# Hybrid decoder trunk on one NeuronCore: another order of the chains around a delta-rule head, and another bank for one part of the mixer's output stage

## The reference

```python
def gated_deltanet_mixer(h, w_in, conv_w, a_log, dt_bias, o_gain, w_out):
    p = h @ w_in
    qkv = jax.nn.silu(causal_depthwise_conv(p[..., :GDN_QKV], conv_w))
    q, k, v = split(qkv);  z, b_logit, a_logit = split(rest of p)
    q = l2_norm(heads_to_chunks(q)) * (GDN_DK ** -0.5)
    k = l2_norm(heads_to_chunks(k))
    ...
    a = strict_lower(kb @ k^T * decay)                  # per chunk
    sol = triangular_solve(a + eye, [v * beta, kb * exp(gc)])
    qk = lower(q @ k^T * decay)
    def step(state, inp):                               # scan over the chunks
        v_new = u_c - w_c @ state
        o = qd_c @ state + qk_c @ v_new
        state = state * cd_c + kd_c^T @ v_new
    o = rms_norm(o, o_gain) * silu(z)
    return o @ w_out
# layer:  x = x + rms_norm(mixer(rms_norm(x)));  x = x + rms_norm(ffn(rms_norm(x)))
```

## Time and profile before

| | |
|---|---|
| time, median of 3 runs | 2989.35 us (2988.05 to 2990.46) |
| time of the profiled execution | 2988.55 us |
| span of its records | 2986.8 us |
| TensorE matmul busy | 2766.5 us (93% of the span) |
| VectorE busy | 1555.9 us (52%) |
| ScalarE busy | 870.7 us (29%) |
| GpSimd busy | 712.1 us (24%) |
| mean granted TensorE clock | 0.965 of full speed |

### The profile page before, as it was taken

The page is one execution under the profiler, slowest core; times in us unless marked ns, Lnnn a source line. Parts: engine busy times, 40 slices in busy tenths (PEclk is TensorE's granted clock), DMA queues, the critical chain, the costliest instruction groups (busy, mean ns, idle before and its releaser), DMA issues. The chain is left out here.

```text
span 2986.8 us, 35606 instructions
## 1 busy us (share of the span) xinstructions
PE 2766.5 (93%) x13277; PEld 2282.7 (76%) x13277; DVE 1555.9 (52%) x1821; ACT 870.7 (29%) x1229; POOL 712.1 (24%) x350
## 2 busy tenths in 40 slices
PE   6789988889889999999998699999989999999996
PEld 4677777778767888888887487787778888888885
DVE  4455545555245445444454675567454444544546
ACT  5244443443433111111111434344531111111112
POOL 2423233333502222222221011111402222222221
PEclk8799999999999999999999799999999999999998
DMA  3010110100332111111111310110521111111112
GB/s 108 22 43 28 35 42 21 42 28 22 113 106 92 43 49 49 42 42 56 49 49 42 128 36 22 49 49 32 169 84 57 45 53 49 49 49 43 49 63 99
DMA packets 59109, 168.04 MB, mean 56 GB/s; under 512 B 6097, under 2 KB 19985, under 8 KB 59041
## 3 DMA queue, kind: packets, MB, share of 16 engines
q1 hardware_dynamic: 59040, 167.14, 16.6%
HBM read 143.49 MB, written 23.63 MB: 56 GB/s over the span
## 5 line engine op out<-in xcount | busy, mean ns | idle before, releaser
L191 POOL TENSOR_TENSOR f_wlo<-f_raw,f_whi 128x1024 fp32r<-128x1024 f32 x130 | 331.2, 2557 | 1101.4 <-ACT f_whi L211 1101.4
L211 ACT ACTIVATE f_whi<-f_raw 128x1024 fp32r<-128x1024 f32 x130 | 137.6, 1058 | 934.1 <-PE f_down L72 425.8
L70 PE MATMUL f_down<-f_whi,f_hhi 128*128 128x512 f32 x704 | 282.7, 402 | 19.5 <-issue 15.6
L250 DVE TENSOR_TENSOR acc<-f_down,acc 128x512 f32<-128x512 f32 x320 | 217.0, 689 | 134.3 <-PE f_down L72 134.3
L70 PE MATMUL banks<-x_hi,f_whi 128*128 128x512 f32 x704 | 276.5, 393 | 10.5 <-PEq L61 10.5
L72 PE MATMUL f_down<-f_whi,f_hlo 128*128 128x512 f32 x704 | 279.4, 397 | 0.0
L71 PE MATMUL f_down<-f_wlo,f_hhi 128*128 128x512 f32 x704 | 278.7, 396 | 0.0
L70 PE MATMUL f_up<-x_hi,f_whi 128*128 128x512 f32 x704 | 276.4, 393 | 2.1 <-POOL f_wlo L191 2.0
L71 PE MATMUL f_up<-x_lo,f_whi 128*128 128x512 f32 x704 | 276.2, 392 | 0.0
L72 PE MATMUL f_up<-x_hi,f_wlo 128*128 128x512 f32 x704 | 276.1, 392 | 0.0
L71 PE MATMUL banks<-x_lo,f_whi 128*128 128x512 f32 x704 | 275.8, 392 | 0.0
(11 more groups left out here) (433 smaller groups left out, 5476.1 us busy)
## 6 DMA issues: line engine op xcount, KB each, us to landing
f_raw<-in_ffn_w_up SPq DMA_DIRECT2D x88, 512.0 KB, 3.5
f_raw<-in_ffn_w_down SPq DMA_DIRECT2D x44, 512.0 KB, 3.5
g_raw<-in_gdn_w_in SPq DMA_DIRECT2D x32, 512.0 KB, 3.5
l_raw<-in_gla_w_in SPq DMA_DIRECT2D x24, 512.0 KB, 3.5
after_ffn_xt<-x_mid SPq DMA_DIRECT2D x16, 512.0 KB, 4.3
first_xt<-in_x SPq DMA_DIRECT2D x8, 512.0 KB, 8.0
g_columns<-cum_rows SPq DMA_DIRECT2D x8, 512.0 KB, 3.9
g_outraw<-in_gdn_w_out SPq DMA_DIRECT2D x8, 512.0 KB, 6.8
```

The lines of the kernel that those rows point to most:

```text
L70: pe.matmul(out, w_hi, x_hi, start=first, stop=False)
L191: pool.tensor_tensor(w_lo[k][:, :], raw[k][:, :], w_hi[k][:, :].bitcast(F32), ALU.subtract) \
L211: act.activation(w_hi[slot(c)][:, :], raw[slot(c)][:, :], ACT.Copy).then_inc(s_hi, 1)
L250: dve.tensor_tensor(part, down_ps[b % 4][:, :], part, ALU.add).then_inc(s_free, 1)
```

## The change

Two things are changed. In the DeltaNet's heads, the output chain of head h-1 is put ahead of the query chain of head h on every engine. On ScalarE the Silu of q leaves the scan and stands after the copy and squares of the scan's output; the last eviction of a head (`evict(h-1, 3, 1)`, the second half of the tile that the fourth projection writes, a Silu of the gate z) stands behind the first chunk's copy of the next scan; the Square of the queries and the high part of weight 3 stand behind the scaling of the output. On TensorE the turn of the queries leaves the scan and follows the first join. On GpSimd the low part of weight 2 is made ahead of the spreading, in head 0 alone. In the output stage DVE adds all E parts ahead of the first norm, and the fourth part goes to the PSUM place of the second one, after tile E.

```diff
@@ mixer_tail
     def m_ps(t):
         if t < E:
-            return (late_ps, *(x.rearrange("p k t -> p (k t)") for x in turned[::-1]))[t % 3]
+            return (late_ps, *(x.rearrange("p k t -> p (k t)") for x in turned[::-1]))[t if t < 3 else 1]
         return part_ps if (t - E) % 2 == 0 else late_ps
@@ Vector.passes
             def add(t):
-                dve.wait_ge(s_m, t + 1)
+                dve.wait_ge(s_m, t + 1 if t < 3 else t + 2)
@@
             dve.wait_ge(s_kept, 2 * E)
-            add(0)
+            for t in range(E):
+                add(t)
             dve.wait_ge(s_gain, 32)
             for t in range(NT + 2):
-                if t + 1 < E:
-                    add(t + 1)
                 if t <= E:
                     m_normed(t)
@@ Tensor.passes
-            for t in range(E + 1):
+            for t in (*range(min(E, 3)), E, *range(3, E)):
                 pe.wait_ge(s_llo, (KT - early) * (1 if t < NT // 2 else 2))
                 if 3 <= t < E:
-                    pe.wait_ge(s_add, 2 * (t - 2))
+                    pe.wait_ge(s_add, 2 * (t - 1))
...
                 if t == E + 1:
-                    pe.wait_ge(s_add, 2 * E)
+                    pe.wait_ge(s_add, 2)
@@ gdn, GpSimd
             def body(h):
                 split(h, 1)
                 near_blocks(h)
+                if peeled(h):
+                    split(h, 2)
                 spread(h, 0)
                 spread(h, 1)
                 coupling(h, 0)
-                split(h, 2)
+                if not peeled(h):
+                    split(h, 2)
@@ gdn, ScalarE, scan
-                              5: lambda: evict(h, 1, 0),
-                              6: lambda: silu(qT, 3 * h + 2)}
+                              5: lambda: evict(h, 1, 0)}
                 for n in range(NT):
...
+                    if n == 0 and projects and not peeled(h):
+                        evict(h - 1, 3, 1)
                     if n in beside:
                         beside[n]()
-                if projects:
-                    act.wait_ge(s_qtok, h + 1)
-                    act.activation(wTn[:, :, :], by_chunk(pm), ACT.Square).then_inc(s_qsq, 1)
-                    evict(h, 1, 1)
-                    if not final(h):
-                        high(h, 3)
@@ gdn, ScalarE, prepare
                 if not peeled(h):
                     output_copy(h - 1)
+                    output_squares(h - 1)
+                silu(qT, 3 * h + 2)
+                evict(h, 1, 1)
                 m1_copies(h, 0)
-                if not peeled(h):
-                    output_squares(h - 1)
-                act.wait_ge(s_qss, h + 1)
-                act.activation(stdq[:, :], ssq[:, :], ACT.Sqrt, bias=eps[:, 0:1]).then_inc(s_qstd, 1)
                 if not peeled(h):
                     output_deviation(h - 1)
                     output_norm(h - 1)
+                act.wait_ge(s_qtok, h + 1)
+                act.activation(wTn[:, :, :], by_chunk(pm), ACT.Square).then_inc(s_qsq, 1)
+                if not final(h):
+                    high(h, 3)
+                act.wait_ge(s_qss, h + 1)
+                act.activation(stdq[:, :], ssq[:, :], ACT.Sqrt, bias=eps[:, 0:1]).then_inc(s_qstd, 1)
                 evict(h, 2, 0)
...
                     key_deviation(h + 1)
-                    evict(h, 3, 1)
@@ gdn, VectorE, prepare
+                if not peeled(h):
+                    output_sums(h - 1)
+                    output_norm(h - 1)
+                join(h, 0)
+                dve.wait_ge(s_silu, 3 * h + 2)
+                dve.tensor_tensor(qdT[:, :, :], by_chunk(qT), from_start[:, :, :], ALU.mult).then_inc(s_qd, 1)
                 dve.wait_ge(s_qsq, h + 1)
                 dve.tensor_reduce(out=ssq[:, :], in_=wTn[:, :, :], axis=AX_X, op=ALU.add).then_inc(s_qss, 1)
-                if not peeled(h):
-                    output_sums(h - 1)
-                dve.tensor_tensor(qdT[:, :, :], by_chunk(qT), from_start[:, :, :], ALU.mult).then_inc(s_qd, 1)
-                join(h, 0)
-                if not peeled(h):
-                    output_norm(h - 1)
                 conv_v(h, (1,))
@@ gdn, TensorE
             def queries_by_token(h):
                 pe.wait_ge(s_silu, 3 * h + 2)
-                pe.wait_ge(s_at, h + 1)
@@ prepare
                 pe.wait_ge(s_first, 2 * h + 2)
-                pe.wait_ge(s_qsq, h + 1)
+                pe.wait_ge(s_at, h + 1)
                 coupled(h, 0)
...
                 joined(h, 0)
+                queries_by_token(h)
                 some(17, 18)
                 if not peeled(h):
+                    pe.wait_ge(s_qsq, h + 1)
                     output_turn(h - 1)
                 some(19)
                 if not peeled(h):
                     pe.wait_ge(s_og, h)
+                else:
+                    pe.wait_ge(s_qsq, h + 1)
                 coupled(h, 1)
@@ first_scan, and scan's last chunk
-                queries_by_token(0)
...
-                    if c == NT - 1:
-                        queries_by_token(h)
```

## The result

| | before | changed kernel |
|---|---|---|
| time, median | 2989.86 us (2988.05 to 2990.46, 4 runs) | 2944.17 us (2941.23 to 2947.63, 4 runs) |
| ratio, 95% interval | | 0.9849 [0.9832, 0.9866] |
| span of the profiled execution | 2986.8 us | 2939.5 us |
| first and last scan begin at | 162.20 and 790.03 us | 148.46 and 743.11 us |

The changed kernel is faster by 45.7 us. The forecast was 2945.0 with a range of 2924 to 2966, and it was right. That it is off by only 0.8 us is luck: the four runs of the changed kernel lie 6.4 us apart, and the interval of the ratio is worth 5 us to either side.

The account below looks back on a forecast made before the run. TensorE works nearly throughout, so only its waits and the low clock behind them can give. Six loop heads 24.6, head 7 6.7, head 0 13, output stage 0: 44.3 off 2988.55 gives 2944.3, plus 0.8 to the median: 2945, range 2924 to 2966.

Parts of the forecast that it names:

- First chunk: Start of a loop head's scan: the 1.58 us wait goes, a state wait of 0.8 to 0.95 comes; net -0.63.
- Last chunk and first join: Loop head: a 2.5 us wait for GpSimd's mask replaces 3.16 on ScalarE; the join starts 3.6 us earlier.
- Portion 16: After the first join: TensorE comes at 380.6 and waits for weight 2's low part until 381.15.
- The output turn: Loop head, after portions 17 and 18: the 3.67 us wait before the output's turn is gone.
- a sign of being wrong: At the second join: a wait over 5 us or stretched GpSimd operations; or clock at 0.50 over 10 us a head.
- step 5: Loop head's second join: squares, high part 3, low part 3, mask, one convolution meeting; 3.1 us wait, start 5.8 us earlier.
- Clock: Low clock behind the new waits of 2.5 and 3.1 us: 2.0 us a head charged, 0.3 given back.
- neither rival on the clock: New waits keep the clock and meet no DVE operation, 2921, chance 0.12; low clock takes back most, 2973, chance 0.16.
- Head 7: Last head, no weight 3: only DVE's gate of the output holds TensorE; 8.2 less 1.5 for clock, 6.7 us gained.
- Head 0: Low part's wait goes, 8 us comes before the second join at 118; query-key products at 131.5; gain 13, bounds 8 and 17.
- The prediction's terms from 118 on: Head 0: second join and products 5.3, low clock 2.3, DVE 0.7, third join, products and portion 5.7 us.
- Output stage: TensorE starts tile 5 earlier but waits longer for DVE's chain of norms: gain 0, between -2 and +1 us.

Follow-up runs that it names:

- Experiment 5: The changed kernel with the gate's second-half eviction back at its old place on ScalarE, ahead of the first chunk's copy: 2950.18 us, ratio 0.9870.
- experiment 6: The changed kernel with GpSimd's second mask moved ahead of low part 3: 2938.11 us, ratio 0.9826.
- experiment 8: The changed kernel with the output gate ahead of the first value convolution on VectorE, alone: 2936.21 us, ratio 0.9828.
- Experiment 10: The kernel of experiment 9 with GpSimd's first mask held back, except in head 0, until ScalarE evicted the queries' second half: 2908.92 us, ratio 0.9729.
- experiment 2: The changed kernel with the output stage of before, so the heads' part of the change alone: 2944.99 us, ratio 0.9852.
- experiment 3: The kernel before with one edit: in head 0 GpSimd makes the low part of weight 2 ahead of the spreading: 2974.44 us, ratio 0.9950.
- experiment 4: The changed kernel without head 0's early low part of weight 2 on GpSimd: 2958.56 us, ratio 0.9892.
- experiment 1: The kernel before with only the output stage's part of the change: 2990.6 us, ratio 1.0003.
- experiment 9: The changed kernel with GpSimd's first mask ahead of both spreads, second ahead of low part 3, and VectorE's output gate ahead of the first value convolution: 2918.24 us.

## Why the prediction was right

By its own steps, before the last scan: 46.92 us gained (790.03 to 743.11), 44.3 forecast. The numbers in brackets are the forecast's.

1. *First chunk.* The 1.58 us went, and the state came late by 0.65 instead of 0.8 to 0.95. Experiment 5 puts 6.0 us on this step over seven heads.
2. *Last chunk and first join.* The wait for the mask is 2.52 us (2.5), on GpSimd, in every loop head.
3. *Portion 16* waits 0.33 us (0.55) for the low part of weight 2.
4. *The output turn* starts at 368.42 with no wait, as forecast.
5. *Second join.* 2.84 us (3.1), at the end of the chain named, with one meeting of GpSimd and VectorE paid: low part 2.38, mask 3.33. Right in size, but thin in its reason. I took the mask for the only thing that held this join in a loop head. Experiments 6 and 8 show that the gate was 1.0 us behind it, so that removing one wait gives only what the other leaves. I had seen the gate for head 7 alone. The prediction named stretched operations of GpSimd at this join as a sign of being wrong, and the mask is stretched, to 3.33 from 2.36 us. By its letter that sign came true; but step 5 had itself charged 1.2 us for one such meeting, and 1.0 was paid, so the sign was worded against the step.
6. *Clock.* Charged 2.0 us a head. The six loop heads average 86.46 us, the one without low clock 84.82: 1.64 a head. That one, head 3, in whose times the steps were worked out, gained 6.24 us, against 5.8 + 0.3 = 6.1 ahead of the clock's charge. The waits of 2.5 and 2.8 us led to it in five heads of six, one or two stretches each, so neither rival on the clock came true. Experiment 10 has neither these waits nor the low clock, and a head takes 80.5 to 80.7 us in it.

A loop head gained 4.50 us on average (27.0 for six, 24.6 forecast): the clock cost less than charged. Head 7 gained 6.16 (6.7), but 2.2 in experiment 2, at another clock, so the agreement there is luck.

*Head 0* gained 13.74 us (13). The second join waits 7.80 us (8) and starts at 117.27 (118); the query-key products start at 131.33 (131.5). The prediction's terms from 118 on add up to 14.0 us and so to 132.0, not 131.5, and the gain to 12.3; measured are 14.06 us. Of its terms the low clock costs 3.0 (2.3), for 6 us of matmuls at 0.50. Experiments 3 and 4 bear out the split between head 0 and the rest: 15.2 and 31 us against 13 and 31.3.

*Output stage*: 0 forecast, 0 measured, in the trace by 21.34 against 21.39 us and in experiment 1 by 1.0003. The chain of norms on VectorE (and ScalarE's deviations in it) decides there, not the tile that TensorE starts earlier.

The part that was wrong is not in the prediction but in what I made of it for experiment 6: that a mask moved ahead gives back the whole wait and the clock behind it. The sum of that was 15 to 25 us, and 6 were there. Nor had I asked where in head 0 the low clock would fall.

What stays open: why one head shows the low clock behind a wait of 2.8 us and the next doesn't. That the head without it is the third in one execution, the fourth in another (experiment 2) and the sixth in a third (the kernel of experiment 4) speaks against a cause in the head itself, but no run shows what it is. The same holds for head 7, whose clock is between 0.93 and 0.99 in these traces.

## What to carry to other kernels

When a wait is named, list everything that the waiting step needs and how long before it each was ready; the second latest is the bound of what removing the latest can give at that wait (here 1.0 of 2.84 us). Where two engines stretch each other's operations, an order in which they meet costs twice, so place the movable one (a mask) where the other is idle, even by an explicit wait. And an earlier start is no gain in itself: in head 0 the later mask was faster by 4 us, since the third join came no later and less work ran at the low clock. Of a long wait ask not only how long it is, but also how much work stands behind it while the clock is low.

## What the runs showed of the hardware

Operations of VectorE and GpSimd held each other up for as long as the other's operation lasted, even tiny ones. In the changed kernel, beside GpSimd's operations from 353.94 to 359.59:

```profile
355.66 1.22 DVE L1804 TENSOR_REDUCE g_sso<-g_inv 128x8 f32<-128x1024 f32 x1 [0.60 <-ACT g_inv L1502]
...
357.38 2.23 DVE L1808 TENSOR_TENSOR g_sso<-g_sso,g_rq 128x8 f32<-128x8 f32 x1
```

The product of 128x8 ended at 359.61, with GpSimd's low part (359.59); its size alone takes 0.17 us, as at L1814. Not every operation is held: the reduction of 128x1024 beside the mask took 1.22, as everywhere, and in experiment 8 the gate, which reads its product from PSUM, took 1.28 us at 365.71, beside a low part from 364.12 to 366.51. A TENSOR_SCALAR of 128x256 took 1.90 us beside GpSimd's low part in head 0, to 85.61, and 0.35 elsewhere. The Trainium skill (SBUF — State Buffer, section SBUF: two separate sides) makes this an exclusive lock held for a whole instruction; the trace agrees for these operations, in both directions (GpSimd's mask 3.33 us instead of 2.36).

TensorE's granted clock stayed at 1.00 behind waits of 2.2 us in five loop heads of experiment 9, and was at 0.50 for a stretch behind one or both of the waits of 2.5 and 2.8 us in five loop heads of the changed kernel. Behind a wait of 6.5 us (experiment 6) the matmuls ran at 0.50 for 12 us, behind one of 7.8 us (changed kernel) for 6 us.
